# A two-layer diffusion trunk on one core: first modulations by picks, next layer's first weights split in the experts

## The reference, cut to what matters

```python
sc, scc = silu(c), silu(c_ctx)
for l in range(2):
    mod   = sc  @ ada_w[l] + ada_b[l]      # 6 x 1024 numbers, for the latent tokens
    mod_c = scc @ ada_w[l] + ada_b[l]      # the same for the context tokens
    sh1, sc1, g1, sh2, sc2, g2 = split(mod, 6)
    h = rmsnorm(x, norm1_g[l]) * (1 + sc1) + sh1
    P = h @ w_in[l]                        # F (256 columns), Q, K, V (512 each), conv, gates
    x = x + g1 * merge(fourier(P), attention(P), conv(P)) @ w_o[l]
    h2 = rmsnorm(x, norm2_g[l]) * (1 + sc2) + sh2
    x = x + g2 * experts(h2)               # 16 experts, two of them for each token
```

## Time and profile before

| | us |
|---|---|
| median of 3 runs (lowest, highest) | 3509.64 (3507.22, 3513.16) |
| the profiled execution, its own time | 3508.45 |
| its span in the trace | 3506.7 |
| PE busy, PEld busy | 3251.4 (93%), 2442.3 (70%) |
| DVE, ACT, POOL busy | 1445.1, 899.6, 796.5 |

### The profile page before, as it was taken

The page is one execution under the profiler, slowest core; times in us unless marked ns, Lnnn a source line. Parts: engine busy times, 40 slices in busy tenths (PEclk is TensorE's granted clock), DMA queues, the critical chain, the costliest instruction groups (busy, mean ns, idle before and its releaser), DMA issues. The chain is left out here.

```text
span 3506.7 us, 46603 instructions
## 1 busy us (share of the span) xinstructions
PE 3251.4 (93%) x16210; PEld 2442.3 (70%) x16211; DVE 1445.1 (41%) x2214; ACT 899.6 (26%) x1696; POOL 796.5 (23%) x512
## 2 busy tenths in 40 slices
PE   6999989999999978999999899889999996899996
PEld 4886567777777865767666787577777775666664
DVE  3465446411112565434450664165111156766412
ACT  2311036311111322222222431055111132222221
POOL 0050000011111125444443022000111123455442
PEclk8999989999999989999999899999999997999998
DMA  5126643111113227757675422142111332989664
GB/s 232 52 85 250 250 147 108 51 36 33 38 32 152 96 102 279 244 171 235 237 269 165 167 76 91 54 143 86 41 48 43 125 130 104 366 321 346 217 180 132
DMA packets 156813, 520.49 MB, mean 148 GB/s; under 512 B 30960, under 2 KB 81776, under 8 KB 131056
## 3 DMA queue, kind: packets, MB, share of 16 engines
q1 hardware_dynamic: 120544, 455.31, 34.8%
q0 software_dynamic: 18432, 62.96, 7.6%
q10 hardware_dynamic: 17712, 0.54, 0.3%
HBM read 432.21 MB, written 86.87 MB: 148 GB/s over the span
## 5 line engine op out<-in xcount | busy, mean ns | idle before, releaser
L216 PE MATMUL wide<-part,part 128*128 128x512 f32 (+2 forms) x2416 | 994.1, 411 | 52.8 <-DVE part L856 15.9
L218 PE MATMUL wide<-part,part 128*128 128x512 f32 (+2 forms) x2416 | 933.3, 386 | 0.0
L217 PE MATMUL wide<-part,part 128*128 128x512 f32 (+2 forms) x2416 | 931.7, 386 | 0.0
L216 PEld LDWEIGHTS wide<-part,part 128*128 128x128 f32 x2416 | 461.0, 191 | 183.5 <-issue 77.1
L217 PEld LDWEIGHTS wide<-part,part 128*128 128x128 f32 x2416 | 461.4, 191 | 107.4 <-issue 24.4
L218 PEld LDWEIGHTS wide<-part,part 128*128 128x128 f32 x2416 | 460.3, 191 | 93.2
L2209 PE MATMUL bank<-place,place 128*128 x864 | 379.7, 592 | 0.0
L2297 DVE CAST part<-place 128x2048 fp32r<-128x2048 f32 x128 | 175.6, 1372 | 437.3 <-DMA place<-in_w 430.8
L2299 DVE TENSOR_TENSOR part<-place,part 128x2048 fp32r<-128x2048 f32 x128 | 316.8, 2475 | 4.4
L2209 PEld LDWEIGHTS bank<-place,place 128*128 128x128 f32 x864 | 159.9, 190 | 180.8 <-issue 180.8
L1579 POOL TENSOR_TENSOR place<-place,place 128x512 f32 (+1 forms) x80 | 111.5, 1394 | 741.4 <-DVE place L1557 741.4
(11 more groups left out here) (231 smaller groups left out, 3850.0 us busy)
## 6 DMA issues: line engine op xcount, KB each, us to landing
place<-in_w SPq DMA_DIRECT2D x124, 1024.0 KB, 16.1
place<-in_w SPq DMA_DIRECT2D x34, 2048.0 KB, 10.5
place<-in_ada_w SPq DMA_DIRECT2D x24, 2048.0 KB, 8.9
place<-in_w_gates SPq DMA_DIRECT2D x32, 640.0 KB, 4.0
place<-in_bias SPq DMA_DIRECT2D x96, 192.0 KB, 3.4
x_rows<-place SPq DMA_DIRECT2D x28, 512.0 KB, 2.9
place<-in_w_rows SPq DMA_DIRECT2D x6, 2048.0 KB, 9.2
place<-in_w_gates SPq DMA_DIRECT2D x16, 768.0 KB
```

Of the source, the lines that this page charges most:

```text
L216: pe.matmul(out, left[0], right[0], start=first, stop=False)
L217: pe.matmul(out, left[0], right[1], start=False, stop=False)
L218: return pe.matmul(out, left[1], right[0], start=False, stop=last)
```

## The change

1. Layer 0's first modulations. The four chunks get a PSUM bank each. Partial results (rows 0 and 1 of four groups) are copied by DVE (two groups) and ACT (two groups) to `partial`, whose row 2 holds the bias and row 3 ones. One product with a constant matrix of picks sums the groups, adds the bias (and 1 for the gain) and gives the row in all partitions. DVE multiplies the gain rows by rows of `norm1_g`. `vec` moves to the head of SP's queue; ACT's queue gets `pick` (256 KB), `gain1` (512 KB) and two loads of the bias (4 KB each).
2. Experts of layer 0. DVE splits layer 1's F and V weights in three pieces, makes `scale1`; after the last block PE broadcasts the six rows of the latent tokens and ACT copies them.
3. Start of layer 1. Only six rows (context tokens) are broadcast; ACT measures tile 0 first; DVE starts with update and norm of tile 0; the two context tiles are loaded after the fourth `acc` tile.
4. Regions move so that these fit (weights, rows, the conv stage's high and low parts); `trig` is loaded after x tile 6.

```diff
+def norm_row(s, v, w):
+    return s["place"]((A_ATT + 3072, w_rows_at()[1][1])[w] + v * D, D)
+def norm_columns(s, layer, v, w, h):
+    src = (s["scale1"][:], s["mod"][:, layer, 0:KD, :], s["mod"][:, layer - 1, 5 * KD:6 * KD, :])[v]
+    return [src[:, 4 * h + j, w:w + 1] for j in range(4)]
...
+                sp.dma_start(vec[:], s["a"]["vectors"]).then_inc(s_vec, 16)
+                load_ada(0)
+                load_ada(1)
                 load_x(0)
...
-                for t in range(NTX, NT):
-                    sp.dma_start(X[:, t], s["x_rows"][t * P:(t + 1) * P]).then_inc(s_x[t], 16)
                 used = sp.value_load(...)
...
+                    if t == 3:
+                        for q in range(NTX, NT):
+                            sp.dma_start(X[:, q], s["x_rows"][q * P:(q + 1) * P]).then_inc(s_x[q], 16)
...
+            def modulate(i):
+                pe.wait_ge(s_ada[i], 16)
+                for k in range(KD):
...
+                            mm = pe.matmul(banks[4 + i][32 * j:32 * j + 2, :], s["silu"][:, k, :], weights[i][:, k, :],
+                                           start=k < 4, stop=k >= 4)
+            def pick_rows(n):
+                v, w, h = rows[n]
+                i = 2 * v + h
+                pe.wait_ge(s_part, 2 * i + 2)
+                pe.wait_ge(s_part2, 2 * i + 2)
+                if v:
+                    pe.wait_ge(s_gain, n - 3)
+                pe.matmul(banks[n % 4][:], pick[:, 2 * v + w], partial[:, i], start=True, stop=True).then_inc(s_b, 1)
...
+                modulate(0)
+                modulate(1)
+                pe.wait_ge(s_small, 48)
+                pe.wait_ge(s_bias, 48)
+                for n in range(4):
+                    pick_rows(n)
+                modulate(2)
+                pick_rows(4)
+                modulate(3)
+                for n in range(5, NR):
+                    pick_rows(n)
...
+                copy_partials(0)                       # ACT, layer 0
+                copy_partials(1)
                 measure(0)
+                copy_partials(2)
+                copy_rows(4)
+                copy_partials(3)
+                copy_rows(5)
                 for k in range(KD):
                     round_weights(F, k)
...
+                copy_partials(0)                       # DVE, layer 0
+                copy_partials(1)
+                dve.wait_ge(s_small, 48)
+                for n in range(4):
...
+                    dve.tensor_tensor(gain[w][:, cs], banks[n][:], gain1[:, cs], ALU.mult).then_inc(s_gain, 1)
+                scale(0)
+                copy_partials(2)
+                copy_partials(3)
...
+                dve.tensor_tensor(XN[:, 0], XN[:, 0], shift[0], ALU.add).then_inc(s_xn, 1)
...
+            if not last:                               # experts, PE
+                pe.wait_ge(s_yc, (used + 1) // 2 * 4 + 2)
+                apart(pe, s_tail)
+                pe.wait_ge(s_sc, 2)
+                for n, (v, h) in enumerate(next_rows):
+                    if n >= 2:
+                        pe.wait_ge(s_bc, n - 1)
+                    broadcast_columns(s, pe, norm_columns(s, layer + 1, v, 0, h), banks[6 + n % 2]).then_inc(s_b, 1)
...
+                for i, (c, n, ks) in enumerate(pieces):   # experts, DVE
+                    dve.wait_ge(s_ahead[min(i, 1) + 1], 16)
+                    if i == 1:
+                        dve.wait_ge(s_room, 1)
+                    dve.tensor_copy(hi[:, ks], raw[:, ks]).then_inc(s_nhi, 1)
+                    dve.wait_ge(s_nhi, i + 1)
+                    dve.tensor_tensor(lo[:, ks], raw[:, ks], hi[:, ks].bitcast(F32), ALU.subtract).then_inc(s_nlo, 1)
```

More of the change, by code:

```diff
@@ L325, in arrive_and_project @@
     whi = [part(hi_at[c], KD, width[c]) for c in range(4)]
[L326 to L330, removed]
+    split_at = {F: 0, V: KD, Q: 2 * KD, K: 3 * KD} if layer == 0 else {Q: 0, K: KD}
     trig = place(at, 2, NTX, HD)
     tabs = place(at + 1024, 4, NTX, HD)
[L333 to L336, removed]
+    pick, gain1 = place(at + 1024, 4, P), place(at + 1536, D)
+    at += 3072
+    gain, shift, g2 = ([norm_row(s, v, w) for w in range(2)] for v in range(3))
     junk = place(at + 2 * D, D)
@@ L340, in arrive_and_project @@
     rot = [place(at + 2048 + i * 512, 512) for i in range(2)]
-    at += 3072
+    at = A_ATT + 26624
+    res = [place(at + i * 512, 512) for i in range(4)]
+    partial = place(at, 4, 512)
+    at += 2048
+    gq = place(at + 80, HD)
     ssum = place(at, 2, HEADS)
@@ L449, in broadcast @@
                 v, w, h = rows[n]
[L450 to L455, removed]
+                broadcast_columns(s, pe, norm_columns(s, layer, v, w, h), banks[row_bank[n]]).then_inc(s_b, 1)
             def turn(t):
                 pe.wait_ge(s_xn, t + 1)
+                if layer and t == 1:
+                    pe.wait_ge(s_bc, NR)
                 if t >= 2:
@@ L523, in round_weights @@
             def round_weights(c, k):
-                if k == 0 and (layer == 0 or c in (Q, K)):
+                if k == 0:
                     act.wait_ge(s_w[c], 16)
@@ L530, in copy_rows @@
                 act.wait_ge(s_b, n + 1)
[L531 removed]
+                act.activation((gain, shift, g2)[v][w][:, h * 512:(h + 1) * 512], banks[row_bank[n]][:], ACT.Copy)\
                     .then_inc(s_bc, 1)
@@ L601, in _ @@
                         round_weights(V, k)
+                if layer and t == 0:
+                    measure(1)
                 if t + 2 < NT:
@@ L682, in _ @@
             else:
-                scale_gain()
-                for c in (F, V):
-                    for k in range(KD):
-                        leave_weights(c, k)
                 update(0)
+                norm(0)
                 update(1)
-                norm(0)
             for t in range(NT):
-                if layer and t + 2 < NT:
+                if layer and 0 < t < NT - 2:
                     update(t + 2)
                 leave_turned(t)
+                if layer and t == 0:
+                    update(2)
                 if t + 1 < NT:
@@ L2281, in _ @@
             used = rounds(act, body)
+            if not last:
+                for n, (v, h) in enumerate(next_rows):
+                    act.wait_ge(s_b, n + 1)
+                    act.activation(norm_row(s, v, 0)[:, h * 512:(h + 1) * 512], banks[6 + n % 2][:], ACT.Copy)\
+                        .then_inc(s_bc, 1)
             for b in range(2):
```

171 lines of the change are left out of this document (100 added, 71 removed).

## The result

The changed kernel's median is 3489.47 us (3488.44 to 3492.22), against 3509.41 (3504.94 to 3513.16) for the kernel before on the same chip: ratio 0.9947 [0.9932, 0.9961], about 20 us faster. The prediction said 3490.8, with a range of 3479 to 3498. The profiled execution took 3491.45, its span is 3489.7 (3506.7 before).

A forecast was written before the change was run, and what follows sets the result against it. PE was busy for 93% of the span, so only its waits, mainly at the two layer starts, could give time: -18.4 - 1.2 + 0.7 = -18.9 from 3508.45, 3489.6, plus 1.2 for the median: 3490.8, range 3479 to 3498.

The forecast's parts named there:

- Layer 0, predicted -18.4: Layer 0's start: modulations by picks shorten the chain to the first product by 18.4 us, bounds 15.5 to 23.5.
- Picks from 22.1 to 28.0: Layer 0's start: picks 0 to 3 follow the copies ending at 22.0 and take 5.9 us, like a broadcast burst.
- Product 3 at the low clock, pick 5 at 1.7: Layer 0's start: after a PE wait, product 3 takes 3.2 to 3.6 us and pick 5 takes 1.7.
- Splits in the experts, predicted 0: Layer 0's experts: DVE's three added pairs, 11.5 us, fit its idle time and add nothing to the path.
- Rival 5: Layer 0's experts: DVE's added pairs delay POOL and so PE by up to 11.5 us, total 3502.3; chance 0.02.
- Broadcasts at the end, predicted +0.7: End of layer 0's experts: six PE broadcasts with a copy, 6.2 to 10.8 us, add 0.7 to the path.
- rival 2: Experts' end: low-clock broadcasts hold the end, costing 4.7 us in place of 0.7, total 3494.8; chance 0.15.
- Start of layer 1, predicted -1.2: Layer 1's start: computation 12.4 us earlier, but tile 0's store lands at 1960.7, so 1.2 saved, bounds 0 to 12.4.
- Rival 1: Layer 1's start: tile 0's store is not held up, saving 12.4 us and not 1.2, total 3479.6; chance 0.13.
- rival 3: Layer 0's start: PE's clock stays low through the whole prologue, saving 15.5 us, total 3493.7; chance 0.1.
- rival 4: Layer 0's start: constants land behind SP's whole stream, picks start at 49.8, 27.7 us later, total 3518.5; chance 0.04.
- Picks that wait for a DMA: Layer 0's start: named sign of being wrong; the forecast had constants landed by 20 and the first pick about 22.

The follow-up runs named there:

- run 5: The changed kernel again, unaltered, as reference on a second chip: 3490.0 us, 0.9944 of the kernel before.
- run 7: Run 6's kernel plus unneeded products filling PE's waits at the starts of layers 0 and 1: 3479.94 us, 0.9909 of the kernel before.
- run 9: Run 6's kernel with layer 1's context tiles loaded after the last acc tile and both stores one acc tile sooner: 3477.68 us, 0.9912 of the kernel before.
- run 3: The changed kernel with layer 1's weights Q asked for after the stores of x tiles 0 and 1: 3484.98 us, 0.9923 of the kernel before.
- run 4: The kernel before the change with the same move of weights Q behind the first two stores: 3511.98 us, 0.9999 of the kernel before.
- run 2: The changed kernel with layer 0's modulations put back as before, leaving experts' end and layer 1's start changed: 3511.25 us, 0.9999 of the kernel before.
- run 6: The changed kernel with stores of x tiles 0 and 1 asked for after the seventh and tenth acc tiles: 3483.1 us, 0.9921 of the kernel before.
- run 8: The changed kernel with all four partial copies of a chunk on DVE, none on ACT: 3495.84 us, 0.9956 of the kernel before.
- Run 1: The changed kernel with experts' end and layer 1's start put back, keeping layer 0's picks: 3489.15 us, 0.9936 of the kernel before.

## Why the prediction was right, and where it was off

**Layer 0, predicted -18.4 (bounds -15.5 to -23.5), measured -24.4.** The mechanism was right and the term mis-sized, a little beyond its outer bound. Three numbers of the sum were off.
- *Picks from 22.1 to 28.0*: they ran from 19.94 to 24.18, 3.8 earlier at the end. The first reads only chunk 0's results, copied at 15.4, so it can follow product 1; the second reads chunk 1's, copied by 21.28. I had put all four behind chunk 1's copies. And they took 4.24 rather than a whole burst of broadcasts (5.94).
- *Product 3 at the low clock, pick 5 at 1.7*: both ran at the high one (1.90, and 2.84 for three picks). PE was idle for only 1.5 us ahead of the last picks, and not before product 3.
- *Copies of chunk 2 behind DVE's gain rows*: right as a mechanism, but they ended at 27.6 and not at 31.8.

So the step of the sum that was mis-sized is the stretch from the first pick to the copy of the last shift rows: 17.9 us predicted (22.1 to 40.0), 14.0 measured (19.94 to 33.89), and begun 2.2 earlier. What followed that copy was 6.8 us (33.89 to 40.68), 6.7 predicted. In this execution the first pick followed product 1 at 19.94, so the constants had come by then, but barely: runs 5, 7 and 9 show PE waiting for the last of them.

**Splits in the experts, predicted 0.** They ran at 1852.6 to 1866.5. That is from 45 us ahead of ACT's last copy of the experts on, where "after 1877" in the kernel before is 46 us ahead of it, so they came when I wrote, and PE stayed full. The windows of the changed kernel:

```profile
1850.00:1870.00 20.00, 20.00 (x82) 13.97 (x81) 12.77 (x8) 5.02 (x9) 11.16 (x5) 1.00 0.59 178
1870.00:1897.00 27.00, 27.00 (x101) 17.39 (x100) 0.00 (x0) 7.28 (x13) 9.86 (x8) 1.00 0.23 51
```

Rival 5 falls with that. POOL was busy for 11.16 of the 20 us, so it had room, and PE never waited for it. Whether DVE shut it out of SBUF for a while, as the Trainium skill has it ("SBUF — State Buffer", "SBUF: two separate sides"), no run here shows.

**Broadcasts at the end, predicted +0.7.** From the start of ACT's last copy to layer 1's first broadcast it took 1908.36 - 1897.73 = 10.6, before 1933.93 - 1923.03 = 10.9. The broadcasts ran at the high clock and their last copy ended at 1904.9, under POOL's add, which landed at 1905.3 (6.0 after its issue; 6.3 in the earlier trace rows). They are hidden, by 0.4 us; the term is 0, and rival 2 is false.

**Start of layer 1, predicted -1.2.** The step on which it rested, that the store of tile 0 takes the place of rows and update as the last wait, is shown by the bracket behind ACT's copy, and by runs 3 and 4: taking Q out of the stream gives 3.9 to 5.1 us after the change and nothing before it. Rival 1 is false. The size: first request for acc to landing of the store was 28.1 us, not 25.8. The DMA engines moved the same 10 MB as before the change (344 GB/s from 1909 to 1938, 382 from 1934 to 1960 in the kernel before), at a lower mean rate; why, no run shows. The two parts in layer 1 come to between -2.0 (run 2) and +0.75 (first profile), with -0.4 in run 5, where I had -0.5 in all. The working of the store's landing in the prediction also falls short of its row: 1957.2 + 1.3 is 1958.5, and the store landed at 1959.9, so 1.4 us of its lateness had no term. The Trainium skill ("DMA: Bandwidth & Descriptors", "Queues, rings and completion order") says that each DMA engine takes the descriptors of one ring in order. The runs agree with it: the store took 14.4 us with Q, the tables and acc tiles ahead of it, 10.4 behind seven tiles (run 6), and 6.3 in run 9, where it was no longer the releaser.

**Low clock in the whole prologue, rival 3.** False: the granted clock was 0.76 from 17 to 24 and 1.00 from 24 to 36. The Trainium skill ("TensorE: Matmul & The Clock Gate", Part 1) calls the low rate the default that activity lifts. The trace agrees in kind: the rate rose during the picks (0.75 from 14 to 20, 0.95 from 20 to 24). Runs 7 and 8 show the other side: a wait of 2.16 us ahead of the picks, and waits of 3 us ahead of picks 4 and 5, are followed by the low rate.

**Constants late, rival 4.** As it was put, false: the first pick stood at 19.94 and not at 49.8. But its ground, small loads of before that had landed by 16.39, hides a wait. In the kernel before PE's first product stood until 16.39 for the 1 KB of `select` on ACT's queue, as its bracket in the earlier trace rows says:

```profile
L570 ACTq DMA_DIRECT2D ident<-in_consts x1: 450/450/450, 1.2 to 1.2; - x1
L571 ACTq DMA_DIRECT2D select<-in_consts x1: 453/453/453, 1.7 to 1.7; - x1
...
DMA to landing us min/median/max: 13.8/14.2/14.6
```

In the changed kernel product 0 no longer waits for it and starts at 10.48. The last constants, which I had put at 19, came by elimination at about 19.7 to 20.5 (run 7): on the edge of the path, and on it as soon as product 1 ended earlier. "Picks that wait for a DMA" was one of the signs of being wrong that the prediction named; runs 5, 7 and 9 show it, with waits of 0.9 to 2.2 us and not of 27.7.

**The total.** The forecast of the total was nearer (1.3 us) than its terms, and that was luck: a layer 0 gain 6 us larger than predicted met a remainder that gave some back. The touched stages won about 23.7 in the profiled pair and 24.4 + 0.4 = 24.8 in run 5, the medians 19.9 and 20.4. The untouched stretches vary by 7 to 9 us between executions, so some of the 4 us between them may be that. What the profiles point to is a loss behind the start of layer 1 in the kernels with moved regions: nine of their ten executions took 1547.4 to 1550.4 there, the two with the old addresses 1542.7 and 1544.3. Whether the addresses are the cause was not settled, and the prediction had them at nothing ("cost nothing: addresses move"). Run 1 (layer 0 alone, 23.2 by medians) does not decide it, its interval being as wide as the difference.

## What to carry to other kernels

When a chain of computation is shortened, look up what else the same instruction waits for and when that lands: here one transfer was 1.7 us behind, and so a 13 us shorter chain (transposes 24.0 and not 37.3 after the last copy of the experts) gave nothing until the queue was reordered. A store that the critical path waits for should be asked for as soon as its data is there, ahead of loads that are needed later; a few moved lines in a queue gave some 11 us beyond the change (by the ratios, 0.9944 in run 5 and 0.9912 in run 9). And small steps on PE cost twice: a longer copy between two products also lowered the clock of the next one (run 8). Last, when work is added to raise that clock, look first at what the step behind it waits for.

## What the runs showed of the hardware

- 1.45 us more per copy made the prologue 8.5 us longer, 4.0 of it by the clock alone (run 8: product 3 took 3.57 in place of 1.90, behind a pick that had waited 3.15).
- Small loads on ACT's queue did not stand behind SP's queue, but they were not quick beside it either. In the changed kernel the 4 KB loads of the bias, issued at 5.3 and 5.8, had come by 19.94, while the fourth chunk, asked for on SP's queue at 3.1, landed at 27.6. But in the kernel before the 1 KB of `select` took 14.6 us, in the changed kernel the 512 KB of `gain1` 15.1, and the last of `select` and the bias by elimination as long. The DMA engines were at 1.03 and 440 GB/s from 17 to 24.
- On one queue a 0.5 MB store took 14.4, 10.4 or 6.3 us, by what had been asked for ahead of it (changed kernel, runs 6 and 9).
- Unneeded products lifted the clock (run 7: product 1 in 1.90, not 3.53 as in run 5), but it fell again while PE waited 2.16 us for a load, and the picks took 5.37 in place of 3.67.
